# A two-layer decoder trunk in float32: products of zeros at the start, the first transfers dealt out anew, and the second tile's transposes inside the first tile's group

## The reference, cut to what matters

```python
def mixer_sublayer(x, ...):
    h = rms_norm(x, norm_pre)
    z = h @ w_in
    c_q, c_kv, k_r, u_conv, u_pool, gate_logits = jnp.split(z, split_at, axis=-1)
    ...
    merged = gates[:, :, 0] * y_attn + gates[:, :, 1] * y_conv + gates[:, :, 2] * y_pool
    return rms_norm(merged @ w_mix_o, norm_post)

def ffn_sublayer(x, norm_pre, w_gate, w_up, w_down, norm_post):
    h = rms_norm(x, norm_pre)
    y = (jax.nn.silu(h @ w_gate) * (h @ w_up)) @ w_down
    return rms_norm(y, norm_post)

    for l in range(DEPTH):
        h = h + mixer_sublayer(h, ...)
        h = h + ffn_sublayer(h, ...)
```

## Time and profile before

| what | value |
|---|---|
| median of 3 runs | 853.03 us (851.9 to 855.12) |
| the profiled execution | 852.31 us |
| its span, first to last instruction | 850.5 us |
| PE busy | 807.2 us, 95% of the span |
| DVE busy | 550.9 us, 65% |
| ACT busy | 430.1 us, 51% |
| POOL busy | 88.3 us, 10% |
| DMA, mean over the span | 170 GB/s |

### The profile page before, as it was taken

One profiled execution on the slowest core, in us unless ns is written; L12 is line 12 of the kernel. 1 busy time (PEld: TensorE's weight loads), 2 busy tenths in 40 slices (PEclk: granted clock), 3 DMA queues, 4 the chain that ended last, 5 costly groups with the idle time before them and its releaser, 6 DMA issues.

```text
span 850.5 us, 10273 instructions
## 1 busy us (share of the span) xinstructions
PE 807.2 (95%) x3924; PEld 678.8 (80%) x3924; DVE 550.9 (65%) x770; ACT 430.1 (51%) x607; POOL 88.3 (10%) x112
## 2 busy tenths in 40 slices
PE   4999799989989999999989979999899999999997
PEld 3898688878768888888869968888777788888885
DVE  4598698869565555554466967887786555555444
ACT  4576455645364444443364664555545544444432
POOL 3610000013040000000040100000314000000000
PEclk9999899999999999999999999999999999999999
DMA  7562544355447555555545643444455665555551
GB/s 271 185 217 84 186 150 139 135 173 161 161 140 250 180 189 182 188 165 193 171 146 171 205 148 128 145 148 152 142 179 165 203 188 187 184 186 176 187 182 50
DMA packets 41234, 144.44 MB, mean 170 GB/s; under 512 B 4705, under 2 KB 4961, under 8 KB 41185
## 3 DMA queue, kind: packets, MB, share of 16 engines
q1 hardware_dynamic: 40896, 142.34, 50.4%
q0 software_dynamic: 144, 0.92, 0.3%
q10 hardware_dynamic: 144, 0.52, 0.2%
HBM read 142.71 MB, written 1.05 MB: 169 GB/s over the span
## 4 chain that ended last, share of the span: by engine, by line
PE 89%; DVE 4%; ACT 2%; POOL 2%; issue 1%; DMA 1%; SPq 0%; DVEq 0%; ACTq 0%
PE acc L373 27%; PE acc L375 26%; PE acc L374 26%; PE tp L445 4%; ACT w_hi L756 1%; PE misc L608 1%; DVE w_lo L1073 1%; PE misc L624 1%; DMA raw<-weights 1%; POOL w_lo L1421 1%; PE tp L460 1%; DVE gates L1277 1%; DMA pos_i<-pos 1%; DVE tp L1087 0%; PE tp L582 0%
## 5 line engine op out<-in xcount | busy, mean ns | idle before, releaser
L1073 DVE TENSOR_TENSOR w_lo<-raw,w_hi 128x1024 fp32r<-128x1024 f32 (+2 forms) x243 | 299.0, 1234 | 217.3 <-ACT w_hi L756 215.1
L756 ACT ACTIVATE w_hi<-raw 128x1024 fp32r<-128x1024 f32 (+3 forms) x254 | 262.1, 1034 | 338.1 <-PE acc L375 323.3
L373 PE MATMUL acc<-w_hi,xT_hi 128*128 128x512 f32 (+3 forms) x800 | 309.6, 387 | 13.6 <-DVE xT_lo L1094 9.6
L374 PE MATMUL acc<-w_lo,xT_hi 128*128 128x512 f32 (+3 forms) x800 | 302.1, 378 | 0.0
L375 PE MATMUL acc<-w_hi,xT_lo 128*128 128x512 f32 (+3 forms) x800 | 302.1, 378 | 0.0
L373 PEld LDWEIGHTS acc<-w_hi,xT_hi 128*128 128x128 f32 x800 | 151.8, 190 | 44.0 <-issue 9.6
L375 PEld LDWEIGHTS acc<-w_hi,xT_lo 128*128 128x128 f32 x800 | 151.6, 190 | 27.6
L374 PEld LDWEIGHTS acc<-w_lo,xT_hi 128*128 128x128 f32 x800 | 152.0, 190 | 24.6
L373 PE MATMUL acc<-w_hi,hT_hi 128*128 128x512 f32 (+1 forms) x300 | 118.1, 394 | 1.2 <-DVE u_sb L1339 1.2
L375 PE MATMUL acc<-w_hi,hT_lo 128*128 128x512 f32 (+1 forms) x300 | 116.2, 387 | 0.0
L374 PE MATMUL acc<-w_lo,hT_hi 128*128 128x512 f32 (+1 forms) x300 | 116.1, 387 | 0.0
(11 more groups left out here) (129 smaller groups left out, 500.0 us busy)
## 6 DMA issues: line engine op xcount, KB each, us to landing
raw<-weights SPq DMA_DIRECT2D x248, 512.0 KB, 3.3
raw<-weights SPq DMA_DIRECT2D x14, 384.0 KB, 3.6
raw<-weights SPq DMA_DIRECT2D x8, 288.0 KB, 2.9
gain<-gains SPq DMA_DIRECT2D x4, 512.0 KB, 4.9
out_rows<-x_sb SPq DMA_DIRECT2D x4, 256.0 KB, 2.0
const<-consts POOLq DMA_DIRECT2D x1, 896.0 KB, 7.7
x_sb<-x_rows ACTq DMA_DIRECT2D x1, 512.0 KB, 4.9
x_sb<-x_rows SPq DMA_DIRECT2D x1, 512.0 KB, 4.7
```

The lines of the kernel that those rows point to most:

```text
L373: pe.matmul(out, a_hi, b_hi, start=start, stop=False)
L374: pe.matmul(out, a_hi, b_lo, start=False, stop=False)
L756: ins = act.activation(w_hi[:, s, first:end], raw[:, s, first:end], ACT.Copy, scale=by)
L1073: ins = dve.tensor_tensor(w_lo[:, s, 0:width], raw[:, s, 0:width], f(w_hi[:, s, 0:width]), ALU.subtract)
```

## The change

Three things are changed together.

1. PE multiplies zeros: DVE sets the tile `diag` to 0 as its first instruction, and PE issues 7 products of `diag` by itself (128x128 by 128x128, float32, into the bank `misc` 1, which nobody reads) ahead of the first transposes, and 13 behind them. `diag` and `misc` have other uses much later.
2. The first transfers: SP issues x's first tile as two halves, weight units 0 and 1, x's second tile as two halves, and the other units. ACT issues the identity's part of the constants and only columns 0 to 36 of layer 0's parameters. POOL issues the positions at the start and, behind its one unit of `lo`, the other parameters in two transfers (semaphore `rest_in`, for which DVE waits ahead of the first tap) and the rest of the constants. Each engine waits for what it reads alone. Unit 1's `lo` goes from POOL to DVE. At layer 0's entry ACT stores tile 0's hi parts ahead of unit 0, and takes both squares behind tile 1's hi parts.
3. `first_group` (all four entries): for each unit the two hi-by-hi products come first and wait for `hi_done` and `tp_hi` only, then the two with the activation's lo part, then the two with `w_lo`. Tile 1's transposes are issued ahead of unit 3 of tile 0 (ahead of unit 2 at layer 0's entry) and no longer behind it.

```diff
-POOL_LO |= {(0, 1), (0, 3)} | {(l, u) for l in range(1, LAYERS) for u in (0, 1, 3)}
+POOL_LO |= {(0, 3)} | {(l, u) for l in range(1, LAYERS) for u in (0, 1, 3)}
+WARM = (7, 13)
...
         def _(sp):
-            sp.dma_start(x[:, 0, :], x_d[0:P, :]).then_inc(x_in[0], 16)
-            sp.dma_start(const[:, 0:K_ONE], const_d[:, 0:K_ONE]).then_inc(const_in, 16)
-            sp.dma_start(par[:, :, :], par_d).then_inc(const_in, 16)
-            sp.dma_start(pos_i[:, :], pos_d).then_inc(const_in, 16)
+            def load_x(t):
+                for h in range(2):
+                    k = slice(512 * h, 512 * (h + 1))
+                    sp.dma_start(x[:, t, k], x_d[t * P:(t + 1) * P, k]).then_inc(x_in[t][h], 16)
+
+            load_x(0)
...
+                    if l == 0 and u == U_G + 1:
+                        load_x(1)
...
-            pe.wait_ge(const_in, 48)
...
                 def first_group(u0, name, use):
-                    for t in range(TOK):
-                        if t == 1:
-                            x_transposes(l, name, 1)
+                    X = l * len(HI_OF) + HI_OF.index(f"{name}0") + 1
+                    for t in range(TOK):
                         bank_free(t, use)
+                        b = acc[:, t, :]
                         for i in range(4):
+                            if t == 0 and i == (2 if name == "X" and l == 0 else 3):
+                                x_transposes(l, name, 1)
+                            s, kts = (base + u0 + i) % RING, (2 * i, 2 * i + 1)
+                            h = 2 * t + i // 2
                             if i % 2 == 0:
-                                tp_emptied(pe, l, TPN[f"{name}{2 * t + i // 2}"])
+                                pe.wait_ge(tp_hi, X + h)
+                            if t == 0:
+                                pe.wait_ge(hi_done, base + u0 + i + 1)
+                            for j, kt in enumerate(kts):
+                                pe.matmul(b, xT_hi[:, kt, tokens(t)], w_hi[:, s, 512 * j:512 * (j + 1)],
+                                          start=kt == 0, stop=False)
+                            if i % 2 == 0:
+                                tp_emptied(pe, l, TPN[f"{name}{h}"])
+                            for j, kt in enumerate(kts):
+                                pe.matmul(b, xT_lo[:, kt, tokens(t)], w_hi[:, s, 512 * j:512 * (j + 1)],
+                                          start=False, stop=False)
                             if t == 0:
                                 unit_ready(u0 + i)
-                            mm = tok_mm(base + u0 + i, t, [2 * i, 2 * i + 1], 512, [acc[:, t, :]], XT, 0, KD - 1)
+                            for j, kt in enumerate(kts):
+                                mm = pe.matmul(b, xT_hi[:, kt, tokens(t)], w_lo[:, s, 512 * j:512 * (j + 1)],
+                                               start=False, stop=kt == KD - 1)
...
+                def warm(n):
+                    for _ in range(n):
+                        pe.matmul(misc[:, 1, 0:P], diag[:, 0:P], diag[:, P:SEQ], start=True, stop=True)
+
                 if l == 0:
+                    pe.wait_ge(zeros_set, 1)
+                    warm(WARM[0])
+                    pe.wait_ge(const_in, 16)
                     x_transposes(0, "X", 0)
+                    warm(WARM[1])
                 first_group(U_G, "X", "G")
...
         def _(act):
-            act.dma_start(x[:, 1, :], x_d[P:2 * P, :]).then_inc(x_in[1], 16)
+            act.dma_start(const[:, 0:K_ONE], const_d[:, 0:K_ONE]).then_inc(const_in, 16)
+            act.dma_start(par[:, 0, 0:C_CW], par_d[:, 0, 0:C_CW]).then_inc(par_in, 16)
...
                 if l == 0:
-                    entry(U_G, "X", R_X, None, 0, 0, 0)
+                    for h in range(2):
+                        hi_scaled(f"X{h}", xT_hi[:, 4 * h:4 * h + 4, tokens(0)])
+                    his(0, 4)
+                    for h in range(2):
+                        hi_scaled(f"X{2 + h}", xT_hi[:, 4 * h:4 * h + 4, tokens(1)])
+                    for t in range(TOK):
+                        for h in range(2):
+                            act.wait_ge(x_in[t][h], 16)
+                        square(R_X + t, x[:, t, :])
...
         def _(dve):
+            dve.memset(diag[:, :], 0.0).then_inc(zeros_set, 1)
             dve.memset(hcT[:, :, 0:TAPS - 1], 0.0).then_inc(pad_zero, 1)
-            dve.wait_ge(const_in, 48)
+            dve.wait_ge(par_in, 16)
...
+                else:
+                    los(0, 2)
+                    x_parts("X", 1, C_PRE, 2)
...
+                if l == 0:
+                    dve.wait_ge(rest_in, 32)
                 taps(4)
...
         def _(pool):
+            pool.dma_start(pos_i[:, :], pos_d).then_inc(pos_in, 16)
...
-                    lo(1)
                     lo(3)
+                    pool.dma_start(par[:, 0, C_CW:], par_d[:, 0, C_CW:]).then_inc(rest_in, 16)
+                    pool.dma_start(par[:, 1:, :], par_d[:, 1:, :]).then_inc(rest_in, 16)
                     pool.dma_start(const[:, K_ONE:NCONST], const_d[:, K_ONE:NCONST]).then_inc(late_in, 16)
```

More of the change, by code:

```diff
@@ L232, in build @@
         late_in = sem("late_in")
-        x_in = [sem(f"x_in{t}") for t in range(TOK)]
+        par_in = sem("par_in")
+        rest_in = sem("rest_in")
+        pos_in = sem("pos_in")
+        zeros_set = sem("zeros_set")
+        x_in = [[sem(f"x_in{t}{h}") for h in range(2)] for t in range(TOK)]
         setup = sem("setup")
@@ L451, in x_transposes @@
                         if name == "X" and l == 0:
-                            pe.wait_ge(x_in[t], 16)
+                            pe.wait_ge(x_in[t][h], 16)
                         else:
@@ L803, in entry @@
                 def entry(u0, name, n, post, at, r_post, count):
-                    if post:
-                        wide_square(at, r_post, 0, post)
-                    his(u0, u0 + (3 if post else 1))
+                    wide_square(at, r_post, 0, post)
+                    his(u0, u0 + 3)
                     for h in range(2):
                         hi_scaled(f"{name}{h}", xT_hi[:, 4 * h:4 * h + 4, tokens(0)])
-                    if post:
-                        wide_square(at, r_post + 1, 1, post)
-                    his(u0 + (3 if post else 1), u0 + 4)
-                    if post:
-                        x_square(n, 0, count)
-                    else:
-                        act.wait_ge(x_in[0], 16)
-                        square(n, x[:, 0, :])
+                    wide_square(at, r_post + 1, 1, post)
+                    his(u0 + 3, u0 + 4)
+                    x_square(n, 0, count)
                     for h in range(2):
                         hi_scaled(f"{name}{2 + h}", xT_hi[:, 4 * h:4 * h + 4, tokens(1)])
-                    if post:
-                        x_square(n + 1, 1, count)
-                    else:
-                        act.wait_ge(x_in[1], 16)
-                        square(n + 1, x[:, 1, :])
-                if l == 0:
-                    entry(U_G, "X", R_X, None, 0, 0, 0)
+                    x_square(n + 1, 1, count)
+                if l == 0:
+                    for h in range(2):
[7 more added lines that the diff above has]
+                        square(R_X + t, x[:, t, :])
                 else:
@@ L1148, in _ @@
                     post_norm(l - 1, 0, 1)
-                x_parts("X", 0, C_PRE, 0 if l == 0 else None)
-                los(1 if l == 0 else 0, 3)
+                x_parts("X", 0, C_PRE)
                 if l:
+                    los(0, 3)
                     post_norm(l - 1, 1, 1)
-                x_parts("X", 1, C_PRE)
+                    x_parts("X", 1, C_PRE)
+                else:
+                    los(0, 2)
+                    x_parts("X", 1, C_PRE, 2)
                 los(3, 11)
@@ L1369, in _ @@
         def _(pool):
+            pool.dma_start(pos_i[:, :], pos_d).then_inc(pos_in, 16)
             pool.memset(half[:, :], -0.5).then_inc(half_set, 1)
             pool.wait_ge(half_set, 1)
-            pool.wait_ge(const_in, 48)
+            pool.wait_ge(const_in, 16)
+            pool.wait_ge(pos_in, 16)
             linked = [0]
```

## The result

The median went from 853.53 us (4 runs, 851.9 to 855.12) to 839.31 us (4 runs, 838.67 to 839.75): ratio 0.9833, 95% interval 0.9812 to 0.9853. The profiled execution took 839.34 us with a span of 837.5, against 852.31 and 850.5. Forecast were 840.1 and a range of 837.0 to 845.0.

What follows compares the result with a forecast made beforehand. PE, busy 807 of 850.5 us, was taken to bound the kernel outside its gaps. Gains of 9.1 at the later entries and 3.8 at the start, 12.9, take 852.31 to 839.4, median 840.1; range 837.0 to 845.0.

Steps and rivals of the forecast that it cites:

- The later entries, 3 x 3.04: At the three later group entries PE's idle time goes: tile 1 starts 3.04 us sooner at each, 9.1 in all.
- The wait for the second half of x: At the later entries, the second half of x's tile 1 holds PE's transposes from 241.75 to 242.05, 0.3 us.
- Rival C: The reordered later entries give back half, by x's second half or a later wait: 4.5 us less, 844.6; chance 0.10.
- The start, 3.8: At the program's start tile 1 begins at 17.3 against 21.06, a gain of 3.8 us.
- My step: At the start ACT stores unit 0's hi part by 8.6 and units 1 to 3 by 9.7, 10.7 and 11.8.
- The 0.7 us added for the median: Median of the runs taken as 0.7 above the profiled execution: 840.1 instead of 839.4.
- Unit 2's wait: At the start PE waits 1.8 us, from 13.6, for DVE's `w_lo` of unit 2, ready at 15.4.
- my 6.2: At the start zeros and transposes together have the clock's fast level up by 6.2, 5.1 us after the first zeros.
- the soonest case: Clock up at 4.5, after 3.4 us of zeros; zeros end at 8.0, gain at the start 5.1, time 838.8.
- Rival A: Transposes don't count towards the clock's rise: rise at 9.6, gain at the start 2.7, time 841.2; chance 0.25.
- Rival B: Zeros bring no clock: all twenty run slow, rise at 15.3, the start gains nothing, 843.9; chance 0.08.
- rival D: Slower than before: other parameters land late through POOL's queue, halting DVE at its first tap, beyond 50.4; chance 0.02.

Runs made afterwards that it cites:

- Kernel 4: Changed kernel, but at the three later entries tile 1's transposes stand behind unit 3 again, the new product order kept: 846.42 us.
- the repeated run: The changed kernel again, no edit: median 839.57 us; its profiled execution, 841.72 us, is the slowest of the four.
- kernel 6: Changed kernel without the seven products of zeros ahead of the first transposes, the thirteen behind them kept: 841.14 us.
- kernel 1: Changed kernel without any of the twenty products of zeros: 841.34 us.
- kernel 10: The mended start of kernel 8 without the twenty products of zeros: 839.39 us.
- kernel 8: Changed kernel, but at layer 0's entry DVE computes `lo` of units 2 and 3 instead of POOL, and unit 2 is issued before x's second tile: 836.51 us.
- kernel 11: Kernel 8 plus 19 products of zeros in PE's stall ahead of each layer's key transposes: 833.25 us of three executions; the fourth 1369.77.
- kernel 9: Changed kernel with the first transfers and their waits as before the change: 842.32 us.
- (3): Changed start alone: the changed kernel with the old first group at the three later entries: 848.04 us.
- (12): Changed kernel with each tile of x in one transfer of 512 KB instead of two halves: 840.06 us.
- kernel 5: Changed kernel with the seven products of zeros ahead of the transposes, without the thirteen behind them: 840.83 us.

## Why the prediction was right, and where it was not

- **The later entries, 3 x 3.04.** Measured 3.03, 3.38 and 3.04 by the marks, 9.45 in all against 9.1, and 9.7 us in the kernel with them alone. Tile 1 came 6.69 us after the entry's first product, forecast 6.6. The wait for the second half of x was to be 0.3 us and is 0.2. Rival C did not happen.
- **What the rows had not shown: the share of each edit.** I had put the whole 3.04 down to idle time that goes. Kernel 4 splits it: 1.6 to 1.8 us the place of the transposes, 1.4 to 1.6 the order of the products, with the place taken away first.
- **The start, 3.8.** At tile 1 it was 2.98 (21.06 to 18.08), at the next mark 3.55. The 0.6 between is the stall ahead of the keys' transposes, where ACT waited 3.39 us for a weight unit before and 2.69 after; that was not in my sum:

```profile
91.33 1.91 PE L445 MATMUL tp<-const,qk 128*96 128x128 f32 x8 [5.49 <-DVE hT_lo L1094]
...
87.54 1.91 PE L454 MATMUL tp<-const,qk 128*96 128x128 f32 x8 [4.79 <-DVE hT_lo L1127]
```

  The mis-sized term is the landing of the weights. My step ran ACT through units 1 to 3 without a stop, hi at 10.7 and 11.8 for units 2 and 3. They had only landed at 11.67 and 12.95, and were stored at 12.7 and 14.0.
- **Luck in the total.** The span fell by 13.0, and the sum said 12.9. That is closer than its terms: 0.35 too little at the entries, 0.8 too much at the start, and 0.6 from a stall that no term had. The 0.7 us added for the median did not come either: the median is 839.31, the profiled execution 839.34.
- **Unit 2's wait.** Forecast 1.8 us with `w_lo` at 15.4; measured 1.16 and 15.2. For unit 3 no wait was forecast, and there were 0.59 us, since POOL started at 14.18 and needed 3.27, where I had 11.8 and 2.4.
- **The shared stretch of DVE and POOL.** Who starts first keeps its own pace, and the other stretches: DVE first, 1.22 and POOL 3.27; POOL first, 2.37 and DVE 2.32. The Trainium skill's rule ("SBUF — State Buffer", section "SBUF: two separate sides") has the second engine blocked until the first is through. By it DVE in the repeated run would end at 15.46 + 1.22 = 16.7, measured 16.5: the trace agrees. Of operations like these the rule names those with two inputs in SBUF, as `w_lo` has them. Behind its `w_lo` DVE took tile 1's two lo parts, with one input in PSUM, at 1.28, their usual time, while POOL still ran: they were not held, which fits the rule too.
- **The clock.** The level rose at 4.5, sooner than my 6.2, and at 7.4 in the repeated run, in the midst of the second batch. The first is the soonest case of the prediction, for which it had put a gain of 5.1 at the start; measured were 2.98, so there the later landings, and POOL's longer `w_lo` behind them, took 2.1 us. Rival A wanted the transposes to break the rise. In the profiled execution the seven zeros had brought it by themselves before the transposes could count for or against. In the repeated run the transposes were slow throughout (1.97) and the rise came behind them, as rival A had it, but at 7.4 and not at 9.6. Whether transposes count towards a rise, no run here tells: with no zeros ahead they were over after 1.94 us (kernel 6), sooner than any rise. The sentence of the Trainium skill ("TensorE: Matmul & The Clock Gate", section "Part 4: PE-mode transpose") that the full clock does not engage for them does not hold here as it reads: once the level was up, eight took 1.04 us, at 12.13, and not 1.97. Rival B did not happen: the second batch ran at 0.22 a product. Its price, for twenty slow products ahead of the first weight product, was not tested; kernel 1, with none, is another case.
- **The rest of the parameters.** DVE's first tap in the timeline after:

```profile
38.40 1.38 DVE L1171 TENSOR_SCALAR cacc<-hcT,par 128x256 f32<-128x256 f32 x4 [1.89 <-ACT hcT L876]
```

It waits for ACT as in the earlier trace rows, not for a transfer: rival D did not happen.

## What to carry to other kernels

Where one engine is busy 95% of the time, list its waits for first operands and work each entry out against the durations of its neighbours; at the entries this gave the gain to 0.4 us in 9. At this program's start the landings of the weights, more than the engines, set the pace, so read the landing of every unit and not only of the first. And products that only keep the clock were worth some 1.8 us with two waits behind them and 2.9 us without, of which the profiles show 1.2 and 0.6 at the start itself, and next to nothing when they covered half of the gap. Take such a gain from executions of the whole kernel, and several of them, since low stretches of the clock further on come and go.

## What was not expected of the hardware

- A wait of some 2.3 us of PE was followed in some executions by some 3 us at a granted clock of 0.50, and in others, with the same wait, not. PE's wait of 2.33 us for POOL's `csum`, which ends between 174 and 183 us, stands in all fourteen profiled executions, and the low stretch behind it in seven (181.5 to 184.9 in the repeated run). At the start the level fell behind waits of 2.26 us (repeated run) and 2.78 (kernel 4), and held behind 2.55 (kernel 6). Near 180 such a stretch cost 1.1 us (kernel 10 against kernel 8), so this is likely a good part of what separates two executions of one kernel.
- The level does not rise at one time after the first zeros. With the same seven from 1.17 on, it rose at 4.0 (kernel 11), 4.4 (9), 4.5 (changed), 4.9 (8), 6.5 (3), 7.3 (4), 7.4 (repeated run) and 9.4 (12), and in kernel 5, without the second batch, only at 13.8, among the weight products. In kernel 9 the transposes came at 6.55, after 2.05 us of idling, and ran fast (1.09): the level had come with the last of the zeros and outlasted the wait. Then, from 7.8 on, in the batch behind them, the granted clock was low. Its window:

```profile
8.50:9.50 1.00, 1.00 (x6) 1.00 (x6) 0.93 (x3) 1.00 (x3) 0.00 (x0) 0.50 0.99 406
```

So the level was lost again behind that wait, but only 1.2 us after PE had gone back to work.

- The granted-clock column shows nothing of the slow level in the first microseconds ahead of the first rise; only the pitch does. Of a later fall, as in this window, it does.
